# Weight panels fetched into the place of their own remainder, with four places, and a new order at the end of the SSM part

## The reference

```python
def first_block(x, ...):
    for layer in range(2):
        h = rms_norm(x, norm_mix[layer])
        if layer < 1:   # S5: u = h @ w_in, a complex diagonal scan per group, y = gelu(...)
            x = x + s5_mixer(h, ...)          # z = y @ w_glu; z[:, :1024] * sigmoid(z[:, 1024:])
        else:
            x = x + stick_breaking_attention(h, w_q, k_shared, v_shared, w_o)
        x = x + conv_ffn(rms_norm(x, norm_ffn[layer]), w_up, conv_w, conv_b, w_down)
        if layer == 0:
            kv = rms_norm(x, norm_kv) @ kv_w  # keys and values of the second layer
    return rms_norm(x, norm_final)

def second_block(x, ...):
    for i in range(2):
        x = layernorm(DN_ALPHA * x + 0.5 * swiglu(x, w13[i, 0], w2[i, 0]), ln_g[i, 0], ln_b[i, 0])
        y = hybrid_mixer(x, w_in[i], ...)     # sliding attention and gated delta rule, two branches, w_out
        x = layernorm(DN_ALPHA * x + y, ln_g[i, 1], ln_b[i, 1])
        x = layernorm(DN_ALPHA * x + 0.5 * swiglu(x, w13[i, 1], w2[i, 1]), ln_g[i, 2], ln_b[i, 2])
    return x
```

## Time and profile before

| | |
|---|---|
| median of 3 executions | 2101.35 us (2100.43 to 2105.58) |
| the profiled execution | 2100.68 us, span in the trace 2098.9 us |
| TensorE busy | 2050.8 us, 98% |
| VectorE busy | 1425.1 us, 68% |
| ScalarE busy | 1053.1 us, 50% |
| DMA | 342.40 MB, 163 GB/s on the mean |
| `w_hi` roundings | 312, 586.1 us |
| `w_lo` subtractions | 312, 704.5 us |

### The profile page before, as it was taken

How to read it: one execution, slowest core, us unless ns; L and a number is a source line. 1 busy time by engine, 2 the same in 40 slices (tenths; PEclk the granted TensorE clock), 3 DMA queues, 4 the chain that set the end, 5 groups by cost and what they waited for, 6 DMA issues and landing times.

```text
span 2098.9 us, 33501 instructions
## 1 busy us (share of the span) xinstructions
PE 2050.8 (98%) x14464; PEld 1791.9 (85%) x14464; DVE 1425.1 (68%) x1636; ACT 1053.1 (50%) x1245; POOL 86.7 (4%) x101
## 2 busy tenths in 40 slices
PE   8899999999999999999999999999999999899998
PEld 8878888989888898997778789888889977788887
DVE  8967766567765664876677766476569576677654
ACT  5545654655643553556544455345435564444542
POOL 1000000000000000220000000000003100000000
PEclk9999999999999999999999999999999999999999
DMA  8156555436656655564312565656546543135653
GB/s 194 14 191 191 184 191 171 152 110 188 192 192 191 203 190 189 171 220 129 124 42 95 171 217 183 198 182 200 190 158 209 195 130 103 43 121 183 199 191 130
DMA packets 259699, 342.40 MB, mean 163 GB/s; under 512 B 23373, under 2 KB 169382, under 8 KB 259552
## 3 DMA queue, kind: packets, MB, share of 16 engines
q1 hardware_dynamic: 253984, 328.90, 49.2%
q0 software_dynamic: 2896, 9.15, 1.4%
q10 hardware_dynamic: 2672, 2.22, 0.6%
HBM read 338.14 MB, written 2.10 MB: 162 GB/s over the span
## 4 chain that ended last, share of the span: by engine, by line
PE 89%; DVE 7%; ACT 2%; issue 1%; DMA 1%; POOL 0%; SPq 0%; DVEq 0%; ACTq 0%
PE trp L2292 16%; PE acc L2292 13%; PE acc L2067 12%; PE acc L2069 12%; PE acc L2068 12%; PE trp L2067 3%; PE acc L2083 2%; PE acc L2238 2%; PE trp L2069 2%; PE trp L2068 2%; PE acc L2132 1%; PE acc L2388 1%; PE acc L2766 1%; PE trp L2771 1%; PE acc L2090 1%
## 5 line engine op out<-in xcount | busy, mean ns | idle before, releaser
L1282 DVE TENSOR_TENSOR w_lo<-raw,w_hi 128x2048 fp32r<-128x2048 f32 (+1 forms) x312 | 704.5, 2259 | 381.1 <-ACT w_hi L761 379.6
L761 ACT ACTIVATE w_hi<-raw 128x2048 fp32r<-128x2048 f32 (+1 forms) x312 | 586.1, 1879 | 473.4 <-PE acc L2069 196.3
L2292 PE MATMUL trp<-xT,w_hi 128*128 128x512 f32 x960 | 228.2, 390 | 0.0
L2292 PEld LDWEIGHTS trp<-xT,w_hi 128*128 128x128 f32 x960 | 178.2, 188 | 35.7
L2067 PE MATMUL acc<-w_hi,hT_hi 128*128 128x512 f32 x528 | 205.5, 389 | 0.0
L2068 PE MATMUL acc<-w_lo,hT_hi 128*128 128x512 f32 x528 | 205.5, 389 | 0.0
L2069 PE MATMUL acc<-w_hi,hT_lo 128*128 128x512 f32 x528 | 205.4, 389 | 0.0
L2067 PE MATMUL acc<-xT,w_hi 128*128 128x256 f32 x704 | 199.6, 283 | 0.0
L2068 PE MATMUL acc<-xT,w_hi 128*128 128x256 f32 x704 | 199.2, 283 | 0.0
L2069 PE MATMUL acc<-xT,w_lo 128*128 128x256 f32 x704 | 199.2, 283 | 0.0
L2292 PE MATMUL acc<-xT,w_hi 128*128 128x512 f32 x768 | 182.5, 390 | 0.0
(11 more groups left out here) (460 smaller groups left out, 3325.7 us busy)
## 6 DMA issues: line engine op xcount, KB each, us to landing
raw<-in_ffn_w SPq DMA_DIRECT2D x184, 512.0 KB
raw<-in_w_in SPq DMA_DIRECT2D x60, 1024.0 KB
raw<-in_ffn_w_up SPq DMA_DIRECT2D x88, 512.0 KB
raw<-in_ffn_w SPq DMA_DIRECT2D x40, 1024.0 KB
raw<-in_ffn_w_down SPq DMA_DIRECT2D x20, 1024.0 KB
raw<-in_ssm_w_glu SPq DMA_DIRECT2D x16, 512.0 KB
raw<-in_kv_w SPq DMA_DIRECT2D x8, 1024.0 KB
raw<-in_w_branch_a SPq DMA_DIRECT2D x8, 1024.0 KB
```

Of the source, the lines that this page charges most:

```text
L761: A(w_hi[:, p % SPL, 0:kt, :], raw[:, p % RAW, 0:kt, :], ACT.Copy).then_inc(hi_ready, 1)
L1282: V_.tensor_tensor(w_lo[:, p % SPL, 0:kt, :], raw[:, p % RAW, 0:kt, :], w_hi[:, p % SPL, 0:kt, :].bitcast(F32), ALU.subtract).then_inc(lo_ ...
L2292: ins = mm(places(out[n // 2][:, n % 2]), weights[:, p % SPL, k, n * P:n * P + P], tokens_of(k0 + k), start=first and k == 0, stop=last an ...
```

## The change

The two places of `raw` are gone. `w_hi` and `w_lo` have four places each (`SPL` = 4), and `raw` is another name for the memory of `w_lo`: a panel arrives in the place of its own remainder, and the subtraction works in place. The total of places is eight as before. The DMA of panel p now waits for `panel_used`, that TensorE is done with panel p-4; `split_hi(p)` waits for the arrival alone. The splits stay three panels ahead (`AHEAD` = 3), at the same places of the programs.

At the end of the SSM part, all four state groups stand in a row on VectorE, `split_lo(6)` comes after `output_rest(3)`, ScalarE's `split_hi(6)` after the fourth quarter's rounding, and TensorE's `gated_inputs(0)` after `outputs_by_chunk(3)` with `keep_warm(2)` in its old place.

```diff
-RAW, SPL = 2, 3
+SPL, AHEAD = 4, 3
...
-        raw = sb("raw", [P, RAW, PK, PN])
         w_hi = sb("w_hi", [P, SPL, PK, PN], F32R)
+        arrivals = ExitStack()
+        raw = sb("raw", [P, SPL, PK, PN], F32, arrivals)
+        arrivals.close()
         w_lo = sb("w_lo", [P, SPL, PK, PN], F32R)
...
+        def arrived(p):
+
+            return raw_loaded[p % SPL], 32 * (p // SPL + 1)
+
...
-                if p >= RAW:
-                    sp.wait_ge(lo_ready, p - RAW + 1)
+                if p >= SPL:
+                    sp.wait_ge(panel_used, p - SPL + 1)
...
-                act.wait_ge(raw_loaded[p % RAW], 32 * (p // RAW + 1))
-                if p >= SPL:
-                    act.wait_ge(panel_used, p - SPL + 1)
+                act.wait_ge(*arrived(p))
                 kt = panels[p][3]
-                A(w_hi[:, p % SPL, 0:kt, :], raw[:, p % RAW, 0:kt, :], ACT.Copy).then_inc(hi_ready, 1)
+                A(w_hi[:, p % SPL, 0:kt, :], raw[:, p % SPL, 0:kt, :], ACT.Copy).then_inc(hi_ready, 1)
...
-                        split_hi(p + SPL)
+                        split_hi(p + AHEAD)
...
-                if q == 2:
-                    split_hi(6)
+            split_hi(6)
...
-                V_.tensor_tensor(w_lo[:, p % SPL, 0:kt, :], raw[:, p % RAW, 0:kt, :], w_hi[:, p % SPL, 0:kt, :].bitcast(F32),
+                V_.tensor_tensor(w_lo[:, p % SPL, 0:kt, :], raw[:, p % SPL, 0:kt, :], w_hi[:, p % SPL, 0:kt, :].bitcast(F32),
                                  ALU.subtract).then_inc(lo_ready, 1)
...
-                if g == 2:
-                    output_rest(0)
-                    dve.wait_ge(lo_ready, 4)
-                    split_lo(4)
+            output_rest(0)
+            dve.wait_ge(lo_ready, 4)
+            split_lo(4)
             output_rest(1)
             split_lo(5)
             output_rest(2)
+            output_rest(3)
             split_lo(6)
-            output_rest(3)
...
             outputs_by_chunk(2)
-            gated_inputs(0)
+            keep_warm(2)
             outputs_by_channel(2)
             outputs_by_chunk(3)
+            gated_inputs(0)
             gated_inputs(1)
```

More of the change, by code:

```diff
@@ L352, in build @@
         ftab_d = nc.dram_tensor("ftab_d", (HEADS, P, P), F32, kind="Internal").ap()
-        raw_loaded = [sem(f"raw_loaded{i}") for i in range(RAW)]
+        raw_loaded = [sem(f"raw_loaded{i}") for i in range(SPL)]
         hi_ready, lo_ready, panel_used = sem("hi_ready"), sem("lo_ready"), sem("panel_used")
@@ L717, in _ @@
                     hs, n = slice(c * PORTION, (c + 1) * PORTION), PORTIONS * i + c
-                    pool.wait_ge(lo_ready, gemms[f"win{i}"][0][0] + SPL + 2 + c)
+                    pool.wait_ge(lo_ready, gemms[f"win{i}"][0][0] + AHEAD + 2 + c)
                     skew = bass.AP(ftab_d.tensor, P - 1 + c * PORTION * P * P, [[P - 1, P], [P * P, PORTION], [1, P]])
@@ L827, in gate @@
                             ins.then_inc(sem("tap_ready"), 1)
-                        split_hi(gemms[f"up{f}"][j][-1] + SPL)
+                        split_hi(gemms[f"up{f}"][j][-1] + AHEAD)
                         act.wait_ge(sem("conv_ready"), 2 * hn + 2)
@@ L1013, in _ @@
                 if t:
-                    split_hi(gemms["glu"][3][0] + SPL)
+                    split_hi(gemms["glu"][3][0] + AHEAD)
                     wait_filled(act, u)
                 A(hbuf[:, 1, t], A2(u)[:, t, PN // 2:PN], ACT.Sigmoid).then_inc(sem("glu_gate"), 1)
-            split_hi(gemms["glu"][3][1] + SPL)
+            split_hi(gemms["glu"][3][1] + AHEAD)
             tsplit("ffn0", *gain_of("ffn0"))
@@ L1059, in _ @@
             softplus(0)
[L1060 removed]
+            split_hi(gemms["v0"][0][0] + AHEAD)
             values_out(0)
[L1062 removed]
+            split_hi(gemms["v0"][0][1] + AHEAD)
             softplus(1)
[L1064 removed]
+            split_hi(gemms["v1"][0][0] + AHEAD)
             values_out(1)
[L1066 removed]
+            split_hi(gemms["v1"][0][1] + AHEAD)
             for i in range(8):
@@ L1226, in _ @@
                     if lv == 1:
-                        split_hi(gemms[f"brA{i}_0"][0][0] + SPL)
+                        split_hi(gemms[f"brA{i}_0"][0][0] + AHEAD)
                 for t in range(TT):
@@ L1233, in _ @@
                     A(Ys[side(1), t], small_bank(trp[t])[side(1)], ACT.Copy).then_inc(sem(f"Y_copied{t}"), 1)
-                split_hi(gemms[f"brA{i}_0"][0][1] + SPL)
+                split_hi(gemms[f"brA{i}_0"][0][1] + AHEAD)
                 def copied(d, to):
@@ L1294, in gemm @@
                         if p <= last - hold:
-                            split_lo(p + SPL)
+                            split_lo(p + AHEAD)
                     if not first or j:
@@ L1298, in gemm @@
                     if not inside and ps[-1] <= last - hold:
-                        split_lo(ps[-1] + SPL)
+                        split_lo(ps[-1] + AHEAD)
                     if after:
                         after(j, place(name, j))
-                late.extend(range(last - hold + 1 + SPL, last + 1 + SPL))
+                late.extend(range(last - hold + 1 + AHEAD, last + 1 + AHEAD))
             def late_splits():
@@ L1479, in gate @@
                                 .then_inc(sem("conv_ready"), 1)
-                        split_lo(gemms[f"up{f}"][j][-1] + SPL)
+                        split_lo(gemms[f"up{f}"][j][-1] + AHEAD)
                     dve.wait_ge(sem("gate_ready"), hn + 1)
@@ L1727, in _ @@
                 scores(i)
-            split_lo(gemms["v0"][0][0] + SPL)
+            split_lo(gemms["v0"][0][0] + AHEAD)
             softplus(0)
             softplus(1)
-            split_lo(gemms["v0"][0][1] + SPL)
+            split_lo(gemms["v0"][0][1] + AHEAD)
             softplus(2)
             softplus(3)
-            split_lo(gemms["v1"][0][0] + SPL)
+            split_lo(gemms["v1"][0][0] + AHEAD)
             for i in range(4):
                 remainders(i)
-            split_lo(gemms["v1"][0][1] + SPL)
+            split_lo(gemms["v1"][0][1] + AHEAD)
             for i in range(4, 8):
@@ L1868, in _ @@
                         scores(n)
-                    split_lo(side_panel(i, n)[2] + SPL)
+                    split_lo(side_panel(i, n)[2] + AHEAD)
                     if n < 8:
@@ L1880, in _ @@
                 decay(2)
-                split_lo(side_panel(i, 10)[2] + SPL)
+                split_lo(side_panel(i, 10)[2] + AHEAD)
                 decay(3)
@@ L1967, in _ @@
                         scaled_keys(lv - 3)
-                        split_lo((side_panel(i, 11)[2], gemms[f"brA{i}_0"][0][0])[lv - 3] + SPL)
+                        split_lo((side_panel(i, 11)[2], gemms[f"brA{i}_0"][0][0])[lv - 3] + AHEAD)
                 for t in range(TT):
@@ L1975, in _ @@
                     dve.sem_inc(*freed(u))
-                split_lo(gemms[f"brA{i}_0"][0][1] + SPL)
+                split_lo(gemms[f"brA{i}_0"][0][1] + AHEAD)
                 u = use[f"dl{i}"] + 1
@@ L2024, in _ @@
                     V_.tensor_tensor(g, g, trp[2 + t][:, :], ALU.mult).then_inc(sem("a1_gated"), 1)
-                late.extend(p + SPL for p in gemms[f"brA{i}_1"][0])
+                late.extend(p + AHEAD for p in gemms[f"brA{i}_1"][0])
                 tsplit(f"delta_{i}")
@@ L2387, in inputs @@
                         for n in range(4):
-                            ins = mm(out[:, n], raw[:, p % RAW, k, n * P:n * P + P], xf[:, k0 + k, :], start=k0 + k == 0 and n % 2 == 0,
+                            ins = mm(out[:, n], raw[:, p % SPL, k, n * P:n * P + P], xf[:, k0 + k, :], start=k0 + k == 0 and n % 2 == 0,
                                      stop=k0 + k == KT - 1, skip_group_check=True)
```

24 lines of the change are left out of this document (12 added, 12 removed).

## The result

| | before | changed |
|---|---|---|
| median | 2100.89 us (2098.17 to 2105.58, 4 runs) | 2110.45 us (2109.12 to 2113.33, 4 runs) |
| profiled execution, span | 2100.68 us, 2098.9 us | 2109.49 us, 2107.7 us |
| TensorE busy | 2050.8 us | 2053.4 us |

The changed kernel is slower by 0.43%: ratio 1.0043, 95% interval 1.0024 to 1.0062. The forecast was 2106 in a range of 2098 to 2112. The prediction gave 0.57 to a change within 0.3% and 0.38 to slower; 0.43% lies beyond that limit, though the lower end of the interval, 0.24%, does not.

The account below looks back on a forecast made before the run. The chain of waits ran through TensorE for 89% of the span and VectorE for 7%. Profiled 2100.68 + 7.2 (late gemm ends) - 2.3 (end of the SSM part) = 2105.6, 2106.3 on the median; forecast 2106, range 2098 to 2112.

Parts of the forecast that it names:

- SSM end: End of the SSM part: panel 6 fetched early, TensorE's 3.00 us wait for `Bm` goes; -2.3 us, bounds -2.66 and -1.
- Steady state: Streamed gemms: later DMA issue stays within about 7 us of slack, 4 us beside a half panel; cost 0.
- Rival C: Streamed gemms: panels late, evacuations delayed, some 80 columns each lose a tenth; +8, about 2114; chance 0.05.
- rival D: Win stages: fetches go out 2 to 4 us earlier, perhaps 3 us of TensorE waits hang on splits; chance 0.04.
- Ends of `down0`, `down2`, `down4`: Gemm ends: late fetch delays ScalarE's rounding, which stands ahead of the next gemm's activations; +2.0, +2.1, +2.1 us.
- Rival B: Gemm ends: the new stalls don't come, only the SSM part's end changes; 2098.4, on the median 2099; chance 0.13.
- End of `o`: `o` to the second FFN: late fetch of 5.3 us, then rounding, delays the activations; +0.8 us.
- End of `down1` and the others: `down1` to the block's final norm: late rounding, +0.2 us; end of glu and other three staggered norms: 0.
- Rival A: Gemm ends: new stalls lower TensorE's clock, one to three drops or longer arrivals; about 2108 to 2113; chance 0.20.

Follow-up runs that it names:

- the order alone: Kernel before with only the new order at the end of the SSM part, its old places kept: 2098.92 us, ratio 1.0000.
- late fetch: Kernel before with four DMAs (panels 48, 64, 132, 242) also waiting until TensorE is done with the panel four earlier: 2109.47 us, ratio 1.0046.
- places alone: Changed kernel with the old order at the end of the SSM part on VectorE, ScalarE and TensorE: 2109.24 us, ratio 1.0044.
- filled stalls: Changed kernel with useless TensorE products in each of four stalls: with four products 2109.72 us, ratio 1.0048; with two 2104.98 us, ratio 1.0024.

## Why the prediction came out as it did

- **SSM end, -2.3 us.** Measured -2.4 at the end of glu. Right in size, and the mechanism (panel 6 early, the copy no longer behind a fetch) is the one seen. What I credited to both edits together is due to the places: the order alone brought nothing in the end, and with the places it isn't needed.
- **Steady state, 0.** Right: no wait on `w_lo` in the streamed gemms, and the larger steps are confined to named places. Rival C is refuted. The small steps everywhere else sum to -1.0 us; rival D had hoped for some 3 us there.
- **Ends of `down0`, `down2`, `down4`, +2.0, +2.1, +2.1.** Measured waits 1.84, 2.00, 2.14: right in size and in mechanism. The chain (release, fetch 5.1 us, rounding, activations, first product) is shown by two runs of opposite sign: delaying four fetches in the kernel before makes the loss, and taking the rounding out of ScalarE's way removes it. Rival B is refuted.
- **End of `o`, +0.8.** Mis-sized: 2.02. The term took 5.3 us for the fetch in halves; it took 6.7. It isn't the next fetch beside it, since with none beside it, in the kernel before with the late fetch, it took 6.6. The traces give a hint: one packet of another DMA queue, `instruction` (16 KB, 1.0 to 1.1 us), falls into this fetch in the three traces in which it took 6.5 to 6.7 us (changed kernel, places alone, late fetch). In the two with filled stalls that packet starts before the first packet of the fetch, which took 6.0 to 6.1. None falls into the late fetches at the three other ends, with 5.0 to 5.3 us. It can explain about half a microsecond; no run isolates it, and what slowed the fetch isn't settled.
- **End of `down1` and the others, +0.2 in all.** About right: TensorE's eight waits for `xT` in the staggered norms sum to 2.7 us instead of 2.2.
- **Rival A, the clock, 0.20.** It happened: two drops, 2.9 us in the trace, and none in the eight filled stalls. I had the pieces (an idle stretch of 1.83 us ahead of a drop in the trace of before) and weighed one counterexample, the 3.00 us gap, too high: the same wait did have a drop behind it in two of the three traces that have it. With the drops counted, 2106 + 1.2 (for `o`) + 2.9 = 2110, close to the measured median of 2110.45. That it fits so well is partly luck: the sum leaves out +1.4 in the delta rule and -1.0 of small steps, and the number of drops is that of one execution (mean clock 0.996; the other three had 0.994 to 0.995). What I held likeliest, 2103 to 2109 without a drop, did not come; the time lies in rival A's range, 2108 to 2113.

## What to carry to other kernels

When a transfer is gated by a later event than before, look not for who needs its data but for what stands behind the instruction that takes the data up: on an engine with a strict order, a copy for work three panels ahead delayed activations that were due at once. Where places are released late, put such a copy behind the urgent work. And a stall of 2 us on TensorE should be priced with a drop of its clock that may follow: here 8 of 12 such stalls had one behind them, at about 1.5 us each in the changed kernel.

## What the runs showed of the hardware

A stall of 1.8 to 2.2 us between stretches of dense products was followed by 3.4 us at half clock (6.8 us in one case) in 8 of 12 cases; in the changed kernel a drop cost about 1.5 us. The same four places kept the full clock when 1.88 or 3.60 us of products without use stood in the stall. This agrees with the Trainium skill ("TensorE: Matmul & The Clock Gate", Part 1), that activity is what keeps the throttle released. The stall's length alone doesn't decide: a wait of 3.00 us for `Bm` had no drop behind it in one trace, and the same wait at 3.17 and 2.22 us had one in two others. I had not expected the same place to come out either way from one kernel to the next.
